# Two reorderings in the stage behind attention: the second pair's cumulative sums on TensorE, its first decays on ScalarE

## The reference, cut to what matters

```python
def compress(kv, j):
    blocks = kv[:, blk_idx] + cmp_pe[j][None, None, :, None, :]
    ...
    return jax.nn.gelu(blocks @ cmp_w1[j] + cmp_b1[j]) @ cmp_w2[j]

kc, vc = compress(k_cmp, 0), compress(v_cmp, 1)
...
p_c = masked_softmax(jnp.einsum('bgiqd,bgkd->bgiqk', qb, kc) + bias_c, dist_c >= 0)
o_c = jnp.einsum('bgiqk,bgkd->bgiqd', p_c.astype(vc.dtype), vc)
```

```python
Lmat = jnp.exp(segsum(A))
scores = jnp.einsum('bclhn,bcshn->bhcls', Ch, Bh) * Lmat
y_diag = jnp.einsum('bhcls,bcshp->bclhp', scores, X)
```

## Time and profile before

| | us |
|---|---|
| median of 3 runs | 3656.82 |
| lowest and highest run | 3651.94, 3661.17 |
| the profiled execution, device time | 3657.5 |
| its span, first to last instruction | 3655.7 |
| its mean granted TensorE clock | 0.993 |

### The profile page before, as it was taken

How to read it: one execution, slowest core, us unless ns; L and a number is a source line. 1 busy time by engine, 2 the same in 40 slices (tenths; PEclk the granted TensorE clock), 3 DMA queues, 4 the chain that set the end, 5 groups by cost and what they waited for, 6 DMA issues and landing times. The chain is left out here.

```text
span 3655.7 us, 43309 instructions
## 1 busy us (share of the span) xinstructions
PE 3561.3 (97%) x17744; PEld 2933.0 (80%) x17744; DVE 1975.7 (54%) x3041; ACT 1227.5 (34%) x1928; POOL 150.9 (4%) x212
## 2 busy tenths in 40 slices
PE   7999999999999999999999999999999999999999
PEld 6888777678888888777678887788788878878887
DVE  6555665775456645665663355666322366553233
ACT  3222334532233222334532223635322355442222
POOL 1110100001000100100000001000000000000000
PEclk8999999999999999999999999999999999999999
DMA  7654331245433644331144331211334222113322
GB/s 268 230 184 128 83 102 41 71 154 190 143 128 110 219 161 128 83 96 47 55 131 126 106 136 48 79 38 53 92 94 126 98 48 75 41 53 104 104 98 81
DMA packets 438041, 397.74 MB, mean 109 GB/s; under 512 B 53779, under 2 KB 390275, under 8 KB 437844
## 3 DMA queue, kind: packets, MB, share of 16 engines
q1 hardware_dynamic: 413028, 310.53, 27.9%
q0 software_dynamic: 24816, 84.45, 6.8%
HBM read 390.14 MB, written 4.78 MB: 108 GB/s over the span
## 5 line engine op out<-in xcount | busy, mean ns | idle before, releaser
L163 PE MATMUL m_ps<-m_h_high,ffn_w_high 128*128 128x512 f32 x2100 | 821.7, 391 | 1.0 <-DVE ffn_w_low L170 1.0
L165 PE MATMUL m_ps<-m_h_high,ffn_w_low 128*128 128x512 f32 x2100 | 818.0, 390 | 0.0
L164 PE MATMUL m_ps<-m_h_low,ffn_w_high 128*128 128x512 f32 x2100 | 817.6, 389 | 0.0
L163 PEld LDWEIGHTS m_ps<-m_h_high,ffn_w_high 128*128 128x128 f32 x2100 | 394.8, 188 | 82.6 <-issue 1.1
L165 PEld LDWEIGHTS m_ps<-m_h_high,ffn_w_low 128*128 128x128 f32 x2100 | 394.5, 188 | 82.8
L164 PEld LDWEIGHTS m_ps<-m_h_low,ffn_w_high 128*128 128x128 f32 x2100 | 394.8, 188 | 81.3
L971 ACT ACTIVATE ffn_sil<-m_ps 128x512 f32<-128x512 f32 x132 | 79.1, 599 | 1128.9 <-PE m_ps L165 1128.9
L163 PE MATMUL m_ps<-ffn_w_high,ffn_hid_high 128*128 128x512 f32 x1056 | 411.6, 390 | 0.0
L165 PE MATMUL m_ps<-ffn_w_high,ffn_hid_low 128*128 128x512 f32 x1056 | 410.9, 389 | 0.0
L164 PE MATMUL m_ps<-ffn_w_low,ffn_hid_high 128*128 128x512 f32 x1056 | 410.9, 389 | 0.0
L1011 DVE TENSOR_TENSOR ffn_hid<-ffn_sil,m_ps 128x512 f32<-128x512 f32 x110 | 75.6, 687 | 549.7 <-ACT ffn_sil L971 549.6
(11 more groups left out here) (485 smaller groups left out, 5439.3 us busy)
## 6 DMA issues: line engine op xcount, KB each, us to landing
m_raw<-in_ffn_w SPq DMA_DIRECT2D x176, 512.0 KB, 4.7
ffn_rows<-in_ada_w POOLq DMA_DIRECT2D x128, 512.0 KB, 5.0
ffn_rows<-in_ffn_w SPq DMA_DIRECT2D x88, 512.0 KB, 3.5
m_raw<-in_w_in SPq DMA_DIRECT2D x32, 1024.0 KB, 5.3
m_raw<-in_ffn_w_gate SPq DMA_DIRECT2D x44, 512.0 KB, 3.7
m_raw<-in_ffn_w_up SPq DMA_DIRECT2D x44, 512.0 KB, 4.8
ffn_rows<-in_ffn_w_down SPq DMA_DIRECT2D x44, 512.0 KB, 3.7
m_raw<-in_w_out SPq DMA_DIRECT2D x24, 512.0 KB, 4.7
```

What stands on the lines that cost most here:

```text
L163: pe.matmul(out, sh, mh, start=first, stop=False, skip_group_check=True)
L164: pe.matmul(out, sh, ml, start=False, stop=False, skip_group_check=True)
L165: return pe.matmul(out, sl, mh, start=False, stop=last, skip_group_check=True)
```

## The change

Two lists get another order; nothing else is changed. On PE, `rows(2)` moves ahead of `turn_hidden`, and `rows(3)` ahead of `keys_values`. On ACT, `decays(1, 0)` moves ahead of `probs(0)`.

```diff
             turn_local(1)
+            rows(2)
             turn_hidden()
             states(0, 1)
+            rows(3)
             keys_values()
             scores(0)
-            rows(2)
             states(0, 2)
             scores(1)
-            rows(3)
             turn(0)
...
             high_local(1)
+            decays(1, 0)
             probs(0)
-            decays(1, 0)
             probs(1)
```

## The result

| | before | after |
|---|---|---|
| median, us | 3654.14 (12 runs) | 3672.07 (12 runs) |
| lowest and highest, us | 3651.62, 3661.65 | 3666.53, 3677.52 |
| profiled execution, device time and span, us | 3657.5, 3655.7 | 3667.2, 3665.4 |
| mean granted clock | 0.9937 (75 runs, taken beside the experiments) | 0.9885 (12 runs) |

The ratio is 1.0045, 95% interval 1.0037 to 1.0053: the change makes the kernel slower by 0.45%. (That is the ratio over all the runs; the two medians alone give 1.0049.) The profiled execution after lies at the fast end of its runs.

A forecast was written before the change was run, and what follows sets the result against it. TensorE, busy 97% of the span, was taken as the bound. The profiled 3657.5 us + 1.0 (order) + 4.6 (clock) gave 3663.1, less 0.7 to the median: 3662.5 us, range 3652.5 to 3675.

The forecast's parts named there:

- the low clock stays: Stage behind attention, past turn(0): without a rows(h) there the half clock runs on, 3667.8 to 3701 us; chance 0.21.
- (a): rows(2) ahead of turn_hidden: starts without a new wait, fills the 1.53 us of idle time, turn_hidden 0.63 us later.
- (b): rows(3) ahead of keys_values: adds 2.26 us, so keys_values starts 2.89 us later.
- (c): Chain from keys_values to normalise(0): 2.89 us later against 2.85 of slack; idle time moves to turn(0), +0.1 us.
- (d): DVE behind the chain: weigh(0,3) late, PE's states(1,0) 0.6 us later; +0.5 us a layer, +1.0 in all.
- (e): PE's clock, keys_values to turn(0): halves in both layers instead of one, for about as long as before; +4.6 us.
- rival 2: Half clock runs on past turn(0), over 32 us in both layers together: 3667.8 to 3701 us; chance 0.21.
- The base: Whole kernel before: profiled execution 3657.5 us, median read as holding one half-clock stretch of 4.56 us, in layer 1.
- Rival 3: PE's wait ahead of turn_hidden: filling it is real gain, up to 1.5 us a layer, below 3652.5 us; chance 0.05.

## Why the prediction was right, and which of its sizes was not

The measured 3672.1 lies in the range, on the side that was forecast, but 9.6 us above the forecast and in the part that was given to the rival "the low clock stays", at 0.21. Against before as measured beside it the change cost 17.9 us, where the forecast had 5.7. That the time is inside the range is owed to the half of that rival which the range took in, not to the sum.

**(a) Right.** rows(2) follows on the local turn with no wait, the 1.53 us are gone. It takes 2.16 us, not 2.25, and the next step follows sooner, so turn_hidden is 0.47 us late (20.46 us into the stage in layer 1 against 19.99) instead of 0.63.

**(b), (c) Right in kind.** keys_values is 2.53 us later, counted from the local turn (1794.45 - 1788.81 against 684.60 - 681.49), not 2.89. The idle time moved to turn(0), released by normalise. turn(0) comes 29.74 us into the stage against 30.10: 0.36 earlier, where +0.1 was forecast, since the chain's delay stays under the slack of 2.85. (In (c), 690.22 is the start of DVE's probabilities(0); scores(0) would end at 690.12, which makes the forecast wait 1.7 us and changes nothing else.)

**(d) Right in kind, too large.** +0.13 us a layer, against +0.5. In layer 0 of the kernel with the filled wait, at full clock, states(1,0) does wait for weigh(0,3):

```profile
694.77 1.10 PE L1760 MATMUL m_ps<-a_raw 128*128 128x512 f32 x2 [0.22 <-DVE rest_decay L2016]
```

It starts 32.93 us into the stage, 0.16 later than before (32.77), where +0.6 was forecast. DVE's list behind the chain is late by less than the 2.89 us: weigh(0,3) starts 32.12 us into the stage in layer 1 of the changed kernel, right behind probabilities(1), against 31.40 before, 0.7 later and not 1.1. ScalarE's part cost nothing, as said; the run with its old order shows it.

**(e) Right in mechanism, mis-sized.** The clock falls at the new thin place in both layers of the profile (28.2 and 28.0 us into the stage). The term was +4.6 us: two pieces of 10.2 us for one. Measured are 20.5 and 13.7 us, twice 20.5 in the run with TensorE's order alone, and 38.5 us more at half clock over all runs, where the term had 10.2. So the term that was put at 4.6 us was worth 14 to 17. By the forecast's own signs the profile lies between (e), 7 to 11 us a layer, and rival 2, past outputs(0). Rival 2's price fits: 3653.2 + 0.45 x (20.5 + 13.7) is 3668.6, and that execution took 3667.2. The step that failed is "for about as long as before". The length before was read from a place with rows(2) close behind; of the row that showed it the forecast made a rival's argument, but not the size. The run with rows(3) behind turn(0) shows that this was it: 6.8 us in both layers. With states(1,0), values(0) and states(1,1), which were held against that rival, the clock was back in layer 1 only as they ended (1812.6), and not in layer 0, where it came back within outputs(0) (713.5).

**The base.** The forecast gave before one piece of 4.56 us and read the steps between its first three runs as such pieces. With 75 runs the groups blur, and part of the scatter lies outside the stages, but the direction holds: the 8 runs of before at a mean clock of 0.995 average 3651.1 us, the 25 at 0.993 3656.6.

**Rival 3** fell: of the up to 1.5 us a layer that it gave, 0.36 appeared at turn(0) and nothing at the stage's end. Its gain exists where only one of the sums goes ahead of the turn of the inner layer and the other takes its place (57.84 us).

**Open.** The kernels with extra matmuls spread over the wait, with six of them, and with the wait of before filled stand 3 to 4 us higher in the last column than before and after; with three in one block it is 1 us. For six, 1.9 us of it are the longer stages (60.60 against 59.66, twice); for the others the stages at full clock show 0.3 us at the most, and the rest has no cause on record. Left open too is how far the half clock near the stage's end, seen in the runs with rows(2) alone, with rows(3) behind turn(0) and others, follows from the changes or from chance.

## What to carry to other kernels

A step that is moved into a gap leaves the place where it covered something: add up the slack of that chain before both covers are taken from it. Here one of two equal steps could go ahead for a gain of 1.8 us a stage, and moving the second ahead too lost all of it and 0.1 us more, before the clock. And look at what the busy share hides: the clock fell in pieces of 31-column matmuls that count as fully busy. In this kernel it paid to keep one wide step between two such pieces and one close behind them, because how long the lower clock lasted went with what followed the fall. In the kernels without extra matmuls a fall around the steps that were moved lasted 3.4 to 10.2 us where it reached into a rows(h), and 13.7 or 20.5 us where it did not.

## What the runs showed of the hardware that was not expected

The clock fell without an idle gap worth the name: with rows(2) alone moved, the engine waited 0.18 us from the turn of the inner layer to turn(0), and the clock fell in matmuls of 31 columns. And at the 1.2 GHz level, 10.8 us of instructions without a wait (turn(0), states(0,3), scores(2), states(1,0), values(0), from 1800.7 to 1811.5 in layer 1 after) did not bring the clock back, nor did 14.9 us of them in layer 0 (695.4 to 710.4). With a rows(h) right behind turn(0) it was back within that step, in both layers of that run, 6.8 us after the fall.
